# First shift and scale multiplied out on TensorE, and the first projection in two halves of its contraction

## What is computed

```python
def rmsnorm(x, g):
    y = xf * lax.rsqrt(jnp.mean(xf * xf, axis=-1, keepdims=True) + EPS)
    return y * g
...
c_act = jax.nn.silu(c)
mod = c_act @ w_ada[l] + b_ada[l]
sh1, sc1, g1, sh2, sc2, g2 = split(mod, 6)
h = rmsnorm(x, norm_gains[l, 0]) * (1.0 + sc1) + sh1
y = token_mixer(h, w_in[l], w_out[l], sinks[l], bias_hb)
x = x + g1 * rmsnorm(y, norm_gains[l, 1])
```

## Time and profile before

| | us |
|---|---|
| runs | 786.7, 787.77, 790.63 (median 787.77) |
| profiled execution, its own time | 789.94 |
| its span, first to last instruction | 788.2 |

### The profile page before, as it was taken

The page is one execution under the profiler, slowest core; times in us unless marked ns, Lnnn a source line. Parts: engine busy times, 40 slices in busy tenths (PEclk is TensorE's granted clock), DMA queues, the critical chain, the costliest instruction groups (busy, mean ns, idle before and its releaser), DMA issues.

```text
span 788.2 us, 12072 instructions
## 1 busy us (share of the span) xinstructions
PE 734.8 (93%) x4062; PEld 619.8 (79%) x4062; DVE 517.8 (66%) x764; ACT 450.2 (57%) x724; POOL 44.4 (6%) x77
## 2 busy tenths in 40 slices
PE   0599999789999999989999999999897999999998
PEld 0498966589999886767989777777686888888886
DVE  6877697777877643457657465665747777777443
ACT  1654678666666433355455687554446777777331
POOL 3100100100000100014101000000000000000000
PEclk9899999979999999998999999999997999999999
DMA  8999985257787655534763564544444666656661
GB/s 315 368 330 338 262 278 167 81 150 206 233 240 263 213 187 166 175 117 115 227 189 114 181 187 131 164 125 138 148 123 134 179 188 175 201 175 197 203 196 57
DMA packets 137167, 150.50 MB, mean 191 GB/s; under 512 B 6164, under 2 KB 111783, under 8 KB 137129
## 3 DMA queue, kind: packets, MB, share of 16 engines
q1 hardware_dynamic: 135278, 145.28, 59.9%
q10 hardware_dynamic: 1852, 4.75, 1.7%
HBM read 148.57 MB, written 1.44 MB: 190 GB/s over the span
## 4 chain that ended last, share of the span: by engine, by line
PE 80%; DVE 10%; issue 4%; ACT 3%; DMA 3%; POOL 1%; SPq 0%; POOLq 0%; DVEq 0%; ACTq 0%
PE acc L1363 13%; PE acc L1364 13%; PE acc L1365 13%; PE acc L1355 11%; PE acc L1342 6%; PE acc L1344 6%; PE acc L1343 6%; PE acc L1356 5%; DVE ada_sum L1038 3%; DMA raw<-in_w_ada 2%; PE aux L1331 2%; DVE wl L960 1%; DMA raw<-in_w_out 1%; PE acc L1595 1%; ACT wh L594 1%
## 5 line engine op out<-in xcount | busy, mean ns | idle before, releaser
L960 DVE TENSOR_TENSOR wl<-raw,wh 128x1024 fp32r<-128x1024 f32 x217 | 266.2, 1232 | 149.5 <-ACT wh L594 148.4
L594 ACT ACTIVATE wh<-raw 128x1024 fp32r<-128x1024 f32 x217 | 227.9, 1055 | 125.6 <-PE acc L1365 109.6
L1342 PE MATMUL acc<-xT,wh 128*128 128x256 f32 x440 | 126.9, 288 | 5.5 <-DVE xT L990 4.1
L1355 PE MATMUL acc<-xT,wh 128*128 128x512 f32 x352 | 127.0, 405 | 0.8 <-DVE xT L982 0.8
L1344 PE MATMUL acc<-xT,wl 128*128 128x256 f32 x440 | 126.1, 287 | 0.0
L1343 PE MATMUL acc<-xT,wh 128*128 128x256 f32 x440 | 126.1, 287 | 0.0
L1363 PE MATMUL acc<-wh,xT 128*128 128x512 f32 (+1 forms) x272 | 111.0, 408 | 4.7 <-DVE xT L982 2.6
L1364 PE MATMUL acc<-wl,xT 128*128 128x512 f32 (+1 forms) x272 | 106.5, 391 | 0.0
L1365 PE MATMUL acc<-wh,xT 128*128 128x512 f32 (+1 forms) x272 | 106.3, 391 | 0.0
L1356 PE MATMUL acc<-xT,wl 128*128 128x256 f32 x352 | 100.0, 284 | 0.0
L1342 PEld LDWEIGHTS acc<-xT,wh 128*128 128x128 f32 x440 | 85.9, 195 | 7.5 <-issue 5.9
(11 more groups left out here) (260 smaller groups left out, 877.1 us busy)
## 6 DMA issues: line engine op xcount, KB each, us to landing
raw<-in_w_in SPq DMA_DIRECT2D x66, 512.0 KB, 3.6
raw<-in_w SPq DMA_DIRECT2D x64, 512.0 KB, 3.8
raw<-in_w_ffn_in SPq DMA_DIRECT2D x44, 512.0 KB, 4.1
raw<-in_w_ada SPq DMA_DIRECT2D x27, 512.0 KB, 6.5
raw<-in_w_ffn_out SPq DMA_DIRECT2D x22, 512.0 KB, 4.3
raw_more<-in_w_ada SPq DMA_DIRECT2D x13, 512.0 KB, 7.2
raw<-in_w_out SPq DMA_DIRECT2D x13, 512.0 KB, 4.8
rows_tmp<-in_w_ada ACTq DMA_DIRECT2D x8, 512.0 KB
```

The source lines that it names most:

```text
L594: A(wh[:, s, :], raw_unit, ACT.Copy).then_inc(rounded, 1)
L960: V.tensor_tensor(wl[:, s, :], raw_slot(r), wh[:, s, :].bitcast(f32), ALU.subtract).then_inc(split_ready, 1)
L1342: mm(bank[:, 0:ROWS], wh[:, s, w], hi, start=(kt == 0), stop=False)
L1355: mm(bank[:, :], wh[:, s, w], moving[:, kt, :], start=(kt == 0), stop=False, skip_group_check=True)
```

## The change

PE makes sh1 and sc1 itself, in two halves of 512 columns each. A unit of `w_ada` now holds one block of 128 rows and, of both chunks, the 512 columns of one half. `mod_start` puts the bias into rows 0 and 32 of a bank of PSUM by a product with the identity. `mod_add` makes two products with a single column of c as the stationary operand, 512 columns long, into rows 0 and 32 (even block) or 64 and 96 (odd block). ACT copies the bank (`copy_mod`), and `mod_columns` adds row 0 to row 64 and row 32 to row 96 by a product with `pick`, which gives columns. DVE finishes with two small instructions (`input_scale`). The 16 units use eight slots of their own (memory of `dbias`, `qT`, `kT`, `vall`), the other items keep the ring of six.

The first projection's units 0 to 11 are cut along the contraction. Units 0 to 3 hold four of the eight row blocks for 256 columns of queries and keys (`block_unit`), 4 and 5 the same four blocks of the values (`value_half`), 6 to 11 the other four blocks. So half of `xT` is enough for units 0 to 5. The accumulators stay open in between: `acc[0]` to `acc[3]` and, for the values, `aux[2]` and `aux[3]`. x is loaded after two units of `w_ada`. The second half's sums stand on PE between the units of the first half.

```diff
-    return {5: 1, 6: 1, 7: 1, 8: 1, 9: 1, 10: 1, 11: 1, 12: 1, 13: 1, 14: 1, 15: 1, 16: 1, 17: 2, 18: 2, 19: 2, 20: 3, 21: 3}.get(u, 0)
+    if 5 <= u <= 17:
+        return 1
+    return {18: 3, 19: 3, 20: 3, 21: 2}.get(u, 0)
...
-    order = [("ada", i) for i in range(ADA_FIRST)]
+    order = [("ada", i) for i in range(KT)]
     i = ADA_FIRST
     for u in range(U_UP1):
         order.append(("w", u))
+        if 1 <= u <= 4:
+            order += [("ada", KT + 2 * (u - 1)), ("ada", KT + 2 * (u - 1) + 1)]
...
-BIAS_AFTER = [5, 17]
+BIAS_AFTER = [8, 17]
+X_AFTER = 1
+HALF_UNITS = 6
+
+EARLY_SLOTS = 8
 
 STREAM = first_stream()
-PLACE = {item: place for place, item in enumerate(STREAM)}
+RING_ITEMS = [item for item in STREAM if item[0] == "w" or item[1] >= ADA_FIRST]
+PLACE = {item: place for place, item in enumerate(RING_ITEMS)}
 
...
+                if kind == "ada" and k < ADA_FIRST:
+                    half, kt = divmod(k, KT)
+                    if k >= EARLY_SLOTS:
+                        sp.wait_ge(ada_used, k - EARLY_SLOTS + 1)
+                    sp.dma_start(early_slot(k).rearrange("p (c n) -> p c n", c=2),
+                                 w_ada[:, kt, 0:2 * D].rearrange("p (c n) -> p c n", c=2)[:, :, 512 * half:512 * (half + 1)])\
+                        .then_inc(early_full[k % EARLY_SLOTS], 16)
...
-                elif 8 <= k < 12:
-                    sp.dma_start(slot.rearrange("p (t n) -> p t n", t=2), w_in[:, 2 * (k - 8):2 * (k - 8) + 2, 2 * W_A:3 * W_A]).then_inc(done, 16)
...
+                    half, j = divmod(k, HALF_UNITS)
+                    if j < 4:
+                        sp.dma_start(slot.rearrange("p (t n) -> p t n", t=4),
+                                     w_in[:, 4 * half:4 * half + 4, 2 * P * j:2 * P * (j + 1)]).then_inc(done, 16)
+                    else:
+                        g = 2 * half + j - 4
+                        sp.dma_start(slot.rearrange("p (t n) -> p t n", t=2),
+                                     w_in[:, 2 * g:2 * g + 2, 2 * W_A:3 * W_A]).then_inc(done, 16)
...
-                if place == 0:
-                    sp.wait_ge(ada_zeroed, 2)
-                    sp.dma_start(ada_sum[0:1, 0:2 * D], a["b_ada"][:, 0:2 * D]).then_inc(ada_bias, 16)
-                if place == 2 * RING - 1:
+                if (kind, k) == ("ada", X_AFTER):
                     for r in range(RT):
-                        sp.dma_start(x[:, r, :], x_dram[:, r, :]).then_inc(x_loaded, 16)
...
+                    sp.wait_ge(ada_used, ADA_FIRST)
...
+            def copy_mod(half):
+
+                act.wait_ge(ada_used, KT * (half + 1))
+                A(mod_rows[:, 512 * half:512 * (half + 1)], mod_bank(half)[:, :], ACT.Copy).then_inc(mod_copied, 1)
...
+            act.wait_ge(ada_zeroed, 1)
+            for c in range(2):
+                act.dma_start(mod_bias[32 * c:32 * c + 1, :], a["b_ada"][:, D * c:D * (c + 1)]).then_inc(ada_bias, 16)
...
+            for r in range(RT):
+                act.wait_ge(x_loaded[r], 16)
+                square_rows(N_IN1, r)
+            for r in range(RT):
+                act.wait_ge(rstd_ready, r + 1)
+                A(xr[:, r, :], x[:, r, :], ACT.Copy, scale=rstd[:, N_IN1, r:r + 1]).then_inc(normed, 1)
...
+            copy_mod(0)
+            round_static(0)
+            from_transposed_half(0, A1, sh1)
+            round_static(1)
...
+            for u in range(4, 7):
+                round_static(u)
+            copy_mod(1)
+            from_transposed_half(1, A1, sh1)
...
-            for i in range(ADA_FIRST):
-                ada(i)
...
+            def input_scale(half):
+
+                dve.wait_ge(mod_psum, half + 1)
+                cols = slice(4 * half, 4 * half + 4)
+                bank = mod_bank(half)[:, 0:8].rearrange("p (t c) -> p t c", c=2)
+                V.tensor_copy(modT[:, M_SH1 + 4 * half:M_SH1 + 4 * half + 4], bank[:, :, 0])
+                V.scalar_tensor_tensor(out=A1[:, cols], in0=bank[:, :, 1], scalar=1.0, in1=vT[:, V_N0 + 4 * half:V_N0 + 4 * half + 4],
+                                       op0=ALU.add, op1=ALU.mult).then_inc(mod_ready, 1)
...
+            input_scale(0)
             low_static(0)
-            split_both(X_PROJ1, {5: 1, 7: 2})
+            split_both(0)
+            low_static(1)
+            for u in range(2, HALF_UNITS + 1):
+                low_static(u)
+            input_scale(1)
+            split_both(1)
+            dve.wait_ge(c_ready, 1)
             dve.wait_ge(misc_loaded, 16 * 3)
             V.tensor_scalar(nsink[:, :], sinks[:, :], -1.0, None, ALU.mult).then_inc(nsink_made, 1)
             dve.wait_ge(ada_bias2, 16)
-            for k in range(12):
-                low_static(k + AHEAD)
-                for i in ada_units_after(k + AHEAD):
+            for i in ada_units_after(HALF_UNITS - 1) + ada_units_after(HALF_UNITS):
+                ada(i)
+            for u in range(HALF_UNITS + 1, 12 + AHEAD):
+                low_static(u)
+                for i in ada_units_after(u):
                     ada(i)
...
+            def mod_start(half):
+
+                mm(mod_bank(half)[:, :], ident[0:33, :], mod_bias[0:33, 512 * half:512 * (half + 1)], start=True, stop=False,
+                   skip_group_check=True)
+
+            def mod_add(i):
+
+                half, kt = divmod(i, KT)
+                pe.wait_ge(early_full[i % EARLY_SLOTS], 16 * (i // EARLY_SLOTS + 1))
+                for c in range(2):
+                    row = 64 * (kt % 2) + 32 * c
+                    ins = mm(mod_bank(half)[row:row + 1, :], cT[:, kt:kt + 1], early_slot(i)[:, 512 * c:512 * (c + 1)], start=False,
+                             stop=kt >= KT - 2, skip_group_check=True)
+                ins.then_inc(ada_used, 1)
+
+            def mod_columns(half):
+
+                pe.wait_ge(mod_copied, half + 1)
+                for t in range(4):
+                    lo = 512 * half + P * t
+                    ins = mm(mod_bank(half)[:, 2 * t:2 * t + 2], mod_rows[:, lo:lo + P], pick[:, :], start=True, stop=True)
+                ins.then_inc(mod_psum, 1)
+
             def sums_to_rows(sums):
...
+            pe.wait_ge(ada_bias, 32)
+            mod_start(0)
+            pe.wait_ge(c_ready, 1)
+            for i in range(4):
+                mod_add(i)
+            pe.wait_ge(vec_ready, 1)
+            for pair in range(2):
+                to_columns_pair(xr, pair, normed)
+            for i in range(4, KT):
+                mod_add(i)
+            pe.wait_ge(sel_made, 1)
+            mod_columns(0)
...
+            def block_unit(u):
+
+                half, c = divmod(u, HALF_UNITS)
+                s = slot_of(u)
+                pe.wait_ge(split_ready, u + 1)
+                for j in range(4):
+                    kt = 4 * half + j
+                    if c == 0 or half == 1:
+                        pe.wait_ge(xT_ready, 4 * (kt // 2) + 4)
+                    hi, lo = xT[:, kt, 0:ROWS], xT[:, kt, ROWS:]
+                    for b in range(2):
+                        bank = acc[c][:, ROWS * b:ROWS * (b + 1)]
+                        w = slice(2 * P * j + P * b, 2 * P * j + P * (b + 1))
+                        first, last = half == 0 and j == 0 and b == 0, half == 1 and j == 3
+                        mm(bank, wh[:, s, w], hi, start=first, stop=False, skip_group_check=True)
+                        mm(bank, wh[:, s, w], lo, start=False, stop=False, skip_group_check=True)
+                        ins = mm(bank, wl[:, s, w], hi, start=False, stop=last, skip_group_check=True)
...
+            block_unit(0)
+            pe.wait_ge(misc_loaded, 16 * 3)
+            mm(acc[3][0:N_HEADS, 0:DIST], relw[:, :], onehot[:, :], start=True, stop=True).then_inc(dist_done, 1)
+            block_unit(1)
+            block_unit(2)
+            pe.wait_ge(tmpT_done, 8)
+            mod_start(1)
+            for i in range(8, 11):
+                mod_add(i)
+            pe.wait_ge(dist_copied, 1)
+            block_unit(3)
+            for i in range(11, 14):
+                mod_add(i)
+            value_half(4, 0)
+            for i in range(14, 16):
+                mod_add(i)
+            to_columns_pair(xr, 2, normed)
+            mod_columns(1)
+            value_half(4, 1).then_inc(unit_done, 1)
+            value_half(5, 0)
+            pe.wait_ge(mod_ready, 2)
+            to_columns_pair(xr, 3, normed)
+            value_half(5, 1).then_inc(unit_done, 1)
+            for u in range(HALF_UNITS, HALF_UNITS + 4):
+                block_unit(u)
+                if u == HALF_UNITS:
+                    pe.wait_ge(vec2_loaded, 16 * 9)
+                    pe.wait_ge(tmpT_done, X_COUNT)
+                    transpose(aux[0][:, 0:V_ROWS - V_EARLY], vrows2[:, :], V_ROWS - V_EARLY).then_inc(vec_cols, 1)
+            for u in (10, 11):
+                value_half(u, 0)
+                value_half(u, 1).then_inc(unit_done, 1)
 ```

(46 more changed lines are left out.)

146 lines of the change are left out of this document (57 added, 89 removed).

## The result

The changed kernel took 792.2 us (median of 15 runs, 790.42 to 797.09) beside 788.8 us of the kernel before (15 runs): ratio 1.0048, 95% interval 1.0031 to 1.0065. It is 3.8 us slower (2.4 to 5.1), where 785.0 was forecast. The profiled execution is its slowest (797.09, 4.9 above the median), so times behind the first projection are read from it with care, and sizes are taken from the medians and from the experiments' traces.

The account below looks back on a forecast made before the run. PE, busy 93% of the span, was taken as the bound. A start 12.7 us sooner, less 11.1 us added to PE's list, gave -1.7; with -1.1 in attention, -2.8: 785.0 us against the median 787.77, range 780.5 to 793.

Parts of the forecast that it names:

- Behind attention nothing moves, and the offset stays: After attention, to the kernel's end: no time gained or lost, so the change there is zero.
- Transfers later: no further wait: Transfers from about 45 us: some 8 us with nothing loaded, yet w9 in time, no more than 1 us to spare.
- -1.1 from w18: Attention: one `w_ada` transfer ahead of unit 18's instead of two, 1.4 us sooner, counted as 1.1 us gained.
- First product at 23.5: Start: the projection's first product on PE at 23.5 us, 12.7 us sooner than 36.22.
- rival 3: PE's clock stays at 1.2 GHz in the first 20 us; first product 1.9 or 5.8 later, 787 to 793.5, chance 0.15.
- PE's list up to unit 11, 11.1 us: Second half's work, now between PE's units, adds 11.1 us up to unit 11's end, forecast at 71.2 us.
- Four rows at once: One-row products in four rows of a bank run side by side on PE; eight units in the list take 4.3 us.
- Rivals 2 and 4: Rival 2: only two rows run at once, 787.5 us, chance 0.20; rival 4: none overlap, 804, chance 0.07.
- Unit 7's wait, 2.1: Before unit 7, PE waits 2.1 us for DVE to take that unit's rest behind columns, A16 and A17.

## Why the prediction was wrong, step by step

- **"Behind attention nothing moves, and the offset stays"**: this step failed, and carries the sign. It looked at the order of work and not at where tiles lie. In the runs `hid` and `yT` lie 32 bytes further, and each of their products takes 7 ns more. That costs 4.1 us in the traces of the FFNs, 0.39% by the two ratios with and without it (1.0048 and 1.0009) and 0.49% in the kernel before. No rival had it.
- **"Transfers later: no further wait"**: failed as well. w9 was indeed the close one, but what costs is that the queue gains nothing back: w9 is issued 4.4 us later than before (56.07, 51.64), and w16 4.7 later (74.98, 70.24). One transfer of `w_ada` goes with each of `w_in`, so six slots hold three units, and a slot's round (transfer, ACT, DVE) takes 8.62 and 8.16 us in the chain above, 2.9 and 2.7 us for a unit. PE takes 2.88, so nothing is gained on it. So w15 and w16 reach ACT late, and ACT's order puts head 0's exponentials behind w16 and DVE's puts w15's rest behind them. With `hid` back unit 11 ends at 71.89, 1.0 sooner than before, and the last sums come at 146.38, 2.5 later: 3.5 us lost in between. With the slot reordered the same stretch (70.88 to 143.30) loses 1.4, so 2.1 hang on that wait in the traces; the two medians (789.54 and 787.95) have intervals that overlap. Where the 1.4 go was not tried.
- **"-1.1 from w18"**: not seen. One transfer of `w_ada` less stands ahead of w18, but the slot for w18 comes free 2.3 later, with w15's rest, so the same late queue and the same wait for head 0's exponentials decide here.
- **First product at 23.5**: 25.53 in the profiled execution, 22.8 to 25.5 over the changed kernel and its nine variants. Transfers were near the forecast (last unit used at 18.24, forecast 17.7). What was left out is the clock, lost at 18.2; rival 3 saw a clock that never rose, the case was one that rose and fell. Ahead of the first product it costs 1.7 us in this execution: the last unit's products take 1.87 and the columns 1.84, with `hid` back, where the clock falls at 21.6, 1.03 and 1.02. In no trace with these waits left empty does it hold; it falls between 18.2 and 24.3. The Trainium skill ("TensorE: Matmul & The Clock Gate", Part 4) says that the full clock doesn't engage for transposes. With 28 of them in the waits the granted clock was 1.00 between 18.5 and 28 us, without them 0.73, so the trace disagrees.
- **PE's list up to unit 11, 11.1 us**: right. With `hid` back, from the first product to unit 11's end it is 47.6 us (24.30 to 71.89), forecast 47.7 (23.5 to 71.2). The changed kernel's own 74.1 has 2.0 of the late start and the clock that fell at unit 7.
- **Four rows at once**: right, and worth 2.55 us of PE's list where 2.5 was forecast; the median moves by 3.4, and the rest isn't explained. Rivals 2 and 4 fall. The Trainium skill ("TensorEngine Tiling (Array Packing)", Theoretical Speedup) allows up to four times for a dimension of at most 32. The trace agrees in that four rows run at once.
- **Unit 7's wait, 2.1**: 1.75 in the trace and, unforeseen, 1.5 more for the clock that fell behind it (unit 7 takes 4.63 us, with `hid` back 3.13). That fall belongs to this execution: with `hid` back and with head 0's slot reordered PE idles 1.76 and 1.75 us at this place and the granted clock stays at 1.00.

In sum: forecast -2.8; the place of `hid` and `yT` adds some 3 to 4, the stretch from unit 11 to the last sums some 3.5 in the traces. That is about the measured 3.8, but the rows don't add up to the last microsecond: with `hid` back the last sums come 2.5 later than before, and the median is 0.7 above (1.0009). With `hid` back and head 0's slot reordered the changed kernel stands at 787.95, 1.2 below the kernel before and within what can be told: the forecast gain of 2.8 is not shown by any run of the change alone.

## What to carry to other kernels

When every product of a stretch takes a few ns more at full clock and with no wait, look at where its operands lie before looking at the schedule: a new small tile moves all tiles behind it, and a pad must be counted in the sizes that the allocator rounds to. A profile in which an early stage got faster and a median that did not are a reason to compare late stages product by product. And a queue that runs at the pace of its consumer, as here from w9 to w16, makes up nothing of a delay. The delay is paid at each later wait in which an engine's program order ties other work to that transfer.
